# A two-layer hybrid decoder step on one core: key and query scaling moved from VectorE to GpSimd, and causal masks of linear attention applied to whole tiles

## The reference, cut to what matters

```
# GLA, inside a chunk: scores with a causal mask, times the values
attn = einsum('bntshk,bnthk,bnshk->bnhts', decay, q, k)      # decay is 0 above the diagonal
o_intra = einsum('bnhts,bnshv->bnthv', attn, v)
# GDN
w     = einsum('bnhts,bnshk->bnthk', t_inv, k * (beta * exp(gam))[..., None])
q_dec = q * exp(gam)[..., None]
k_dec = k * exp(g_last[:, :, None] - gam)[..., None]
# per chunk: v_new = u - w @ s;  o = q_dec @ s + a_qk @ v_new;  s = s * exp(g_last) + k_dec^T @ v_new
```

## Time and profile before

| | |
|---|---|
| runs, median (lowest to highest) | 1939.02 us (1932.7 to 1939.81) |
| profiled execution, its own time | 1937.77 us |
| its span | 1936.0 us |
| mean granted clock of TensorE | 0.978 of full |
| PE busy | 1845.9 us (95%) |
| DVE busy | 1471.4 us (76%) |
| ACT busy | 1100.7 us (57%) |
| POOL busy | 14.3 us (1%), 30 instructions |

### The profile page before, as it was taken

The page is one execution under the profiler, slowest core; times in us unless marked ns, Lnnn a source line. Parts: engine busy times, 40 slices in busy tenths (PEclk is TensorE's granted clock), DMA queues, the critical chain, the costliest instruction groups (busy, mean ns, idle before and its releaser), DMA issues.

```text
span 1936.0 us, 25113 instructions
## 1 busy us (share of the span) xinstructions
PE 1845.9 (95%) x10189; PEld 1534.6 (79%) x10189; DVE 1471.4 (76%) x1834; ACT 1100.7 (57%) x1098; POOL 14.3 (1%) x30
## 2 busy tenths in 40 slices
PE   5998999999999989898999999999999999999996
PEld 2996677999988977766888888878888888788884
DVE  2867758555358768578788888888898888888895
ACT  3855233433337643327667666766767767667673
POOL 0000000000000000000000000000000000000000
PEclk8999899999999998998999999999999999999998
DMA  9446345543466452166999999999998989999990
GB/s 377 162 148 207 120 169 214 222 153 112 135 214 261 137 206 89 61 255 240 347 354 346 335 361 334 343 354 335 353 344 336 363 327 353 352 331 361 340 361 29
DMA packets 92296, 505.30 MB, mean 261 GB/s; under 512 B 8112, under 2 KB 8272, under 8 KB 40848
## 3 DMA queue, kind: packets, MB, share of 16 engines
q1 hardware_dynamic: 89616, 488.29, 68.4%
q0 software_dynamic: 2560, 15.34, 2.1%
HBM read 494.88 MB, written 8.72 MB: 260 GB/s over the span
## 4 chain that ended last, share of the span: by engine, by line
PE 77%; DVE 15%; ACT 4%; DMA 1%; issue 1%; SPq 1%; POOL 0%; DVEq 0%; ACTq 0%; POOLq 0%
PE bank L646 74%; DVE wlo L458 5%; ACT whi L452 1%; DMA raw<-in_w_in 1%; DVE work L1807 1%; PE bank L1152 1%; ACT L1304 1%; ACT work L1304 1%; SPq L581 1%; DVE hT L1712 1%; PE bank L887 1%; DVE y_low L2280 1%; DVE work L1808 1%; ACT wscr L1304 0%; PE bank L1140 0%
## 5 line engine op out<-in xcount | busy, mean ns | idle before, releaser
L458 DVE TENSOR_TENSOR wlo<-raw,whi 128x2048 fp32r<-128x2048 f32 (+1 forms) x412 | 921.1, 2261 | 181.0 <-ACT whi L452 179.7
L452 ACT ACTIVATE whi<-raw 128x2048 fp32r<-128x2048 f32 (+1 forms) x412 | 761.0, 1889 | 87.5 <-PE bank L646 75.7
L646 PE MATMUL bank<-whi,hg_high 128*128 128x512 f32 x896 | 361.9, 404 | 1.5 <-DVE hg_low L2265 1.5
L646 PE MATMUL bank<-wlo,hg_high 128*128 128x512 f32 x896 | 355.6, 397 | 0.0
L646 PE MATMUL bank<-whi,hg_low 128*128 128x512 f32 x896 | 355.4, 397 | 0.0
L646 PE MATMUL bank<-hh,whi 128*128 128x320 f32 x944 | 298.2, 316 | 11.4 <-DVE hl L1724 6.2
L646 PE MATMUL bank<-hh,wlo 128*128 128x320 f32 x944 | 293.0, 310 | 0.0
L646 PE MATMUL bank<-hl,whi 128*128 128x320 f32 x944 | 292.8, 310 | 0.0
L1304 ACT ACTIVATE work<-bank 128x512 f32<-128x512 f32 (+5 forms) x193 | 88.5, 481 | 209.2 <-PE bank L646 186.8
L646 PEld LDWEIGHTS bank<-hh,whi 128*128 128x128 f32 x944 | 178.8, 189 | 29.7 <-issue 16.3
L646 PEld LDWEIGHTS bank<-whi,hg_low 128*128 128x128 f32 x896 | 169.0, 189 | 41.1
(11 more groups left out here) (279 smaller groups left out, 1888.3 us busy)
## 6 DMA issues: line engine op xcount, KB each, us to landing
raw<-in_moe SPq DMA_DIRECT2D x336, 1024.0 KB, 4.8
raw<-in_ada SPq DMA_DIRECT2D x56, 1024.0 KB, 5.3
raw<-in_w_in SPq DMA_DIRECT2D x30, 1024.0 KB, 6.5
raw<-in_gu SPq DMA_DIRECT2D x22, 1024.0 KB, 5.1
raw<-in_down SPq DMA_DIRECT2D x16, 704.0 KB, 4.1
raw<-in_w_out SPq DMA_DIRECT2D x8, 1024.0 KB, 4.9
work<-in_s_gdn POOLq DMA_DIRECT2D x2, 2048.0 KB, 12.7
out_gdn_s<-work POOLq DMA_DIRECT2D x2, 2048.0 KB, 9.2
```

The costliest lines, as they stand in the source:

```text
L452: ac.activation(whi[:, part(n), 0:width(n)], raw[:, slot, 0:width(n)], ACT.Copy).then_inc(S("w_high"), 1)
L458: ve.tensor_tensor(wlo[:, slot, 0:width(n)], raw[:, slot, 0:width(n)], whi[:, part(n), 0:width(n)], ALU.subtract).then_inc(S("w_low"), 1)
L646: return pe.matmul(out, lhsT, rhs, start=start, stop=stop, **k)
```

## The change

GpSimd gets three pieces of VectorE's list, in each layer: `scaled_keys(0)` (two instructions), the decayed queries of tile 0 (one instruction, that of line 2032 for i = 0) and `scaled_keys(1)` (two instructions). They report on a new semaphore `dpool`. VectorE keeps `scaled_keys(2)` and the decayed queries of tiles 1 and 2. New waits: VectorE ahead of `scaled_keys(2)`, whose `DKD` lies over tile 0's `DX`, and in `invert` ahead of the first overwriting of `DU` of tiles 0 and 1; TensorE ahead of `keys(0)`, `keys(1)` and `outputs(0)`. GpSimd's wait for `gla_tr` 3 and the load of `GSS[0]` now stand behind `scaled_keys(0)` and the queries; `scaled_keys(1)` stands behind the store of the GLA state.

`gla_scored(0)` and `(1)` lose the zeroing and their eight strips, and mask with two instructions each that go over all 128 partitions: the even heads' and the odd heads' scores times the triangle. A semaphore `la` is dropped, whose wait in TensorE stood behind that for all projections.

```diff
@@ gpsimd
+                def scaled_keys(i):
+                    nt, DKB, DKD, DU = TILES[i][1], DSET[i][1], DSET[i][2], DSET[i][6]
+                    kn = v3(DU[0:nt, :], 4)
+                    after(po, "dqk", l, 2 * i + 2)
+                    po.tensor_tensor(v3(DKB[0:nt, :], 4), kn, last(gBG[0:nt, 4 * i:4 * i + 4], NK), ALU.mult)
+                    po.tensor_tensor(v3(DKD[0:nt, :], 4), kn, last(gDK[0:nt, 4 * i:4 * i + 4], NK), ALU.mult)\
+                      .then_inc(S("dpool"), 1)
+
+                def scaled_queries():
+                    nt, DX = P, DSET[0][8]
+                    after(po, "drowe", l, 1)
+                    after(po, "dkk", l, 2)
+                    qd = cv3[:, 0:4, 0:nt]
+                    po.tensor_tensor(qd, qd, v3(DX[:, :], 4), ALU.mult).then_inc(S("dpool"), 1)
+
+                scaled_keys(0)
+                scaled_queries()
                 after(po, "gla_tr", l, 3)
                 po.dma_start(GSS[0], A["s_gla"][l, 0, :, :, :]).then_inc(S("gla_state_in"), 16)
                 after(po, "gla_state", l, 2)
                 store(O["gla_p"][l, :, :, :], GS, "gla_out")
+                scaled_keys(1)
@@ tensor
-                after(pe, "la", l, 1)
@@ keys(i)
+                    if i < 2:
+                        after(pe, "dpool", l, DKD_DONE[i])          # DKD_DONE = (1, 3)
@@ outputs(i)
-                    after(pe, "dqd", l, i + 1)
+                    if i:
+                        after(pe, "dqd", l, i)
+                    else:
+                        after(pe, "dpool", l, DKD_DONE[0] + 1)
@@ scalar, squares_qk
-                            after(ac, "dqd", l, i)
+                            after(ac, "dqd", l, 1)
@@ vector, gla_scored(i)
-                    if i == 0:
-                        do(ve.memset(GAT, 0.0))
                     if i < 2:
                         if i:
                             after(ve, "gla_o_mm", l, i)
-                        for j, nj in enumerate(NJ):
-                            r0 = SUB * j
-                            for e in range(2):
-                                ins = tt(v3(GAT, 4)[r0:r0 + SUB, e::2, r0:], v3(GAB[e][:, 0:256], 2)[r0:r0 + SUB, :, r0:],
-                                         mid(cst("tri")[r0:r0 + SUB, r0:], 2), ALU.mult)
-                                go(ins) if (j, e) != (len(NJ) - 1, 1) else do(ins, "gla_at")
+                        for e in range(2):
+                            ins = tt(v3(GAT, 4)[:, e::2, :], v3(GAB[e][:, 0:256], 2), mid(cst("tri"), 2), ALU.mult)
+                            go(ins) if e == 0 else do(ins, "gla_at")
@@ vector, scaled_keys(i), now called for i = 2 alone
+                    after(ve, "dpool", l, DKD_DONE[0] + 1)
@@ vector, first_level(i)
+                    if i == 0:
+                        return
                     qd = cv3[:, 0:4, t0:t0 + nt]
@@ vector, invert, level 0
+                                if i < 2 and hs == 0:
+                                    after(ve, "dpool", l, DKD_DONE[i])
@@ vector, order
                 gla_scored(1)
-                scaled_keys(0)
                 first_level(0)
@@
                 gla_scored(2)
-                scaled_keys(1)
                 first_level(1)
```

More of the change, by code:

```diff
@@ L134 @@
     "conv_done": 1, "conv_in": 16, "conv_out": 16, "cv_e": 12, "cv_raw": 12, "dat": 3, "dkk": 6, "dlog": 3,
-    "dmask": 3, "dmb": 31, "do": 3, "do_mm": 3, "dqd": 3, "dqk": 6, "dqkT": 6, "drow": 3, "drowe": 3, "ds_mm": 2,
+    "dmask": 3, "dmb": 31, "do": 3, "do_mm": 3, "dpool": 3, "dqd": 2, "dqk": 6, "dqkT": 6, "drow": 3, "drowe": 3, "ds_mm": 2,
     "dsq": 6, "dss_mm": 4, "dtb": 6, "dtr": 9, "dtu": 31, "dtu_mm": 26, "dvm": 4, "dvn": 3, "dvn_mm": 3,
@@ L140 @@
     "gla_ktr": 3, "gla_o": 3, "gla_o_mm": 3, "gla_ops": 3, "gla_out": 48, "gla_s_mm": 2, "gla_ss_mm": 4,
-    "gla_sstate": 2, "gla_state": 2, "gla_state_in": 32, "gla_tok": 6, "gla_tr": 3, "gla_vm": 4, "gx": 1, "hl_in": KD, "hl_out": KD, "la": 1,
+    "gla_sstate": 2, "gla_state": 2, "gla_state_in": 32, "gla_tok": 6, "gla_tr": 3, "gla_vm": 4, "gx": 1, "hl_in": KD, "hl_out": KD,
     "out_mm": 8, "proj": 29, "proj_mm": 29, "small_mm": 1, "smallw_in": 16, "x_mix": 8, "xp_ready": 1,
@@ L543, in build @@
         GATHERED = (2, 3, 4)
+        DKD_DONE = (1, 3)
         def md(base, n=KD):
@@ L1839, in _ @@
                         ve.wait_ge(S("vec_own"), own.n["vec_own"])
-                        do(cp(la, LAE), "la")
+                        do(cp(la, LAE))
                         low.to(AT_IN[l] + 5 + LEAD)
```

## The result

The changed kernel takes 1950.87 us (median of 4 runs, 1950.5 to 1954.67) beside 1935.86 for the kernel before (1932.39 to 1939.81): ratio 1.0066, 95% interval 1.0043 to 1.0090. Twelve more runs of the same program, taken later beside 35 of the kernel before, gave 1.0051 (1.0032 to 1.0071). So it is slower by 10 to 15 us. The forecast was 2 us slower, 1932 to 1948.

A forecast was written before the change was run, and what follows sets the result against it. TensorE bounds the kernel (77% of the ending chain); VectorE counts only in the mixer's middle stage, between 158.5 and 187 us. Minus 0.8 plus 2.8 gives 2.0 us slower, median 1939.0 to 1941.0, range 1932 to 1948.

The forecast's parts named there:

- Masks: gla_scored(0) on VectorE: 1.5 us less and the zeroing besides become idle time ahead of normalize(0); gain nothing.
- 3.3 us less on VectorE, of which 0.8 arrive in layer 0: Work removed before normalize(1); TensorE's list frees turn_back(1) only 0.8 us sooner, so strict(1) gains 0.8; layer 1 gains 0.
- The new waits: VectorE's and TensorE's waits for GpSimd: each GpSimd instruction would need over 8 us for one to bind; nothing.
- GSS[0]'s load: GpSimd's load behind three more instructions, the last able to start about 11 us before its existing wait ended; nothing.
- GpSimd's length: Length t of each GpSimd instruction: 0.69 us as lower bound, 2.1 as the far one.
- Interference: keys(0): GpSimd's two instructions beside decays(0) and operands(1) delay strict(0) by 0.69 us each: 1.4 us a layer, 2.8 in both.
- Interference: keys(1) charged at nothing: Ahead of strict(1) VectorE has 2.5 us to spare; at most one instruction hits it, 0 to t, taken as 0.
- The clock counted as 0, 4 either way: TensorE's clock in the middle stage: preceding gaps stay, moved by a microsecond or two; 0, with 4 us either way.
- The slower rival: Long GpSimd instructions hold VectorE, six on the path; at t = 2.1 net 11.8 us slower, 1950.8 us; chance 0.10.
- point of decision, 1.75 us: Instruction length t from which the slower rival, six instructions on the path, passes the 0.5% bound of 9.7 us.
- the bound of 4.4 us: Loss from keys(0) by the skill pages, up to 4.4 us against 0.8 gained, net 3.6 slower, keys(1) left out.

The follow-up runs named there:

- the masks alone: Kernel before with two wide mask instructions a tile in place of zeroing and eight strips, nothing on GpSimd: ratio 0.9995 (0.9975 to 1.0014).
- the late-keys kernel: Changed kernel, but GpSimd's keys of tile i also wait for ScalarE's row decay, so they run behind strict(i): ratio 1.0006 (0.9985 to 1.0027) to the kernel before.
- the second profile: Profile of the unaltered changed kernel when measured again; those runs gave ratio 1.0051 (1.0032 to 1.0071) to the kernel before.
- with the gap filled: TensorE's ada(x,6) moved ahead of turn(2): changed kernel 1.0002, kernel before 0.9979, wide masks with VectorE's tile 1 keys done twice ahead of strict(1) 0.9998.
- the pair split in two: Changed kernel, but GpSimd waits for its first key instruction to end before issuing the second: 1.0011; six runs 1933.51 to 1937.87 us, six 1944.4 to 1946.17.
- the writes: Changed kernel with GpSimd's four key instructions replaced by writes of zeros of the same outputs: ratio 1.0012 (0.9993 to 1.0030) to the kernel before.
- the line moved: ada(x,6) ahead of turn(2) in four kernels: doubled VectorE keys 0.9998, changed kernel 1.0002, kernel before 0.9979, late GpSimd keys 0.9981.

## Why the prediction was wrong, point by point

- **Masks.** Right. Two instructions take 0.76 us together, VectorE's idle time ahead of normalize(0) grew from 0.43 to 2.66 us, and the masks alone give a ratio of 1.
- **3.3 us less on VectorE, of which 0.8 arrive in layer 0.** The mechanism is right: turn_back(1) follows TensorE's own list, and 0.84 us show in the late-keys kernel. In the changed kernel it isn't seen, because turn(1) took 2.23 and its row sums 1.92 us at the low clock.
- **The new waits, and GSS[0]'s load.** Right, nothing. GpSimd issues that load as soon as TensorE's line 786 lets it, with 10.44 us of waiting before it, at 182.32.
- **GpSimd's length.** Taken as 0.69, measured 1.04 when nothing is in its way; inside the bounds of 0.69 and 2.1.
- **Interference: keys(0).** Right in kind and nearly in size: 1.2 us at strict(0) in each layer for 1.4 taken. Alone it costs some 2 us, too little for the runs to tell from nothing.
- **Interference: keys(1) charged at nothing.** The first step that failed. The prediction gave VectorE 2.5 us to spare ahead of strict(1) and let at most one of the two instructions touch it. VectorE did win time, but it lost it at once in gla_carried(1), where it waits 2.03 us for TensorE's state product (179.70, above), a wait that was not looked at (in the other profiles and layers of the same program it is 0.43 to 2.56 us). Behind it only about 1 us was left: ScalarE's masks(1) ended at 185.20 us, strict(1) began at 186.61, so of the hold of 2.4 us 1.4 were uncovered, and as much in layer 1 and in the second profile. And both instructions held it, one after the other. With 1.4 us a layer for keys(1), 1.2 for keys(0) and the 0.8 gained, the sum comes to 4.4 us; with the gap filled, 4.8 are measured.
- **The clock counted as 0, 4 either way.** The second, and at least as large: 5 to 8 of the 10 to 13 us by the ratios. The prediction noticed that a gap of TensorE precedes the fall, and then took the gaps as unchanged, "moved by a microsecond or two". They are not unchanged: TensorE has one more, 1.26 us ahead of gla_scores(2). The runs show that such a microsecond is the expensive one: 1.2 us of extra work ahead of strict(1) costs nothing, 2.4 cost 0.35%, and with the gap filled 2.4 cost some 0.2%. In the profile of the changed kernel 5.5 of the 16.8 us are the stretch behind strict(1) of layer 1, and 3.0 more the start of layer 1's output projection, where ten matmuls took 4.12 us instead of 2.43.
- **The slower rival.** It named 1950.8 us, which is where the median fell, but by a mechanism that is not this one: GpSimd instructions of 2.1 us, all on the path. They take half of that, and of what they hold only 2.6 us a layer are on the path; the low clock pays the other part. Its point of decision, 1.75 us, is wrong, because it left the clock out.

The page that the prediction weighed, the Trainium skill's "SBUF — State Buffer", section "Who interferes with whom", is borne out: products with two SBUF inputs were held behind GpSimd's products (0.69 to 1.18 and 1.41 us) and not behind its writes (0.69), and VectorE's products with one input in PSUM were not held (0.75 for two, and 2.32 for the eight strips). A one-input copy was held behind a write (0.22 to 0.82); the page allows that for copies that take both port pairs, and whether this one does, no row shows. The estimate of 1.1 us from "GPSIMD Engine Reference", section 3.1, stands beside 1.04 measured. By that page and the bound of 4.4 us the sum was still less than half of the loss.

What stays open: which property of TensorE's gaps decides how long the low clock lasts. The kernel before shows 21.2 and 16.7 us for the same stretch in its two layers, and the kernel with the pair split in two ran at two levels some 9 us apart. The profiles say that a filled gap helps; they don't say by what rule. That layer 1's output projection also loses time was not tested: its ten matmuls take 4.12 us in both profiles of the changed kernel, but also in that of the writes and in two of those with the line moved, and 4.03 with the masks alone, and these are as fast as the kernel before or faster. So it isn't shown that the 3.0 us come from the change.

## What to carry to other kernels

Before work is moved to GpSimd, look at what VectorE reads at that moment, not only at whether GpSimd is idle: two instructions of 1.04 us on a free engine stopped the busy one for 1.2 us in one place and for 2.4 in another. Where TensorE stands still for a microsecond or two and the granted clock falls behind it, count a delay ahead of that gap at more than its length (here about twice, once it was longer than the microsecond to spare), and look first for an independent step of TensorE's own list to put into the gap. That one moved line brought a delay back to about its own length, and by itself it made the kernel before 4 us faster. Compare such a repair with the old kernel repaired in the same way, or its own gain hides what is still lost. And when an engine is relieved, follow it to its next wait before calling the time spare.

## What the runs showed of the hardware that was not expected

- Two GpSimd products issued back to back held one VectorE product of 128 x 128, usually 0.28 us, for 2.67 us; with a wait between them it took 1.67. In the other place, decays(0), VectorE's two instructions fell between the two of GpSimd, and GpSimd's second one took 1.47 us instead of 1.04. Why VectorE gets in there and not here is not settled.
- The held VectorE product began at 183.01 and GpSimd's first by its row at 183.47, when the former should have been over: either GpSimd's recorded start is later than the moment from which it holds VectorE, or something ahead of its products holds it already. Which of the two is not known.
- Forty matmuls of the sampled tokens took 8.71 us at the low clock throughout and 5.07 to 6.51 us where it was high for a part of them.
